# First two slots of an in-projection as three f32r products of rounded parts and rests

## The reference

```python
h = rms_norm(x, g_pre_mix[i])
proj = h @ w_in[i]
sb_q, sb_k, sb_v, q_lat, kv_lat, k_rope = jnp.split(proj, split_at, axis=-1)
...
cos, sin = rope_tables(positions, x.dtype)
```

## Time and profile before

| | us |
|---|---|
| median of 3 runs (lowest to highest) | 994.34 (993.92 to 997.03) |
| the profiled execution, its own time | 995.91 |
| the profiled execution, span from first to last instruction | 994.1 |
| PE busy | 813.6 (82%) |
| DVE, ACT, POOL busy | 331.9, 309.9, 143.9 |
| mean granted PE clock | 0.928 |

### The profile page before, as it was taken

How to read it: one execution, slowest core, us unless ns; L and a number is a source line. 1 busy time by engine, 2 the same in 40 slices (tenths; PEclk the granted TensorE clock), 3 DMA queues, 4 the chain that set the end, 5 groups by cost and what they waited for, 6 DMA issues and landing times.

```text
span 994.1 us, 12347 instructions
## 1 busy us (share of the span) xinstructions
PE 813.6 (82%) x5144; PEld 528.1 (53%) x5144; DVE 331.9 (33%) x700; ACT 309.9 (31%) x621; POOL 143.9 (14%) x153
## 2 busy tenths in 40 slices
PE   7998879999999999999889998767666775665854
PEld 5856447899997886687768542213112221221212
DVE  3306465667676545559531310001000000100001
ACT  2316355666665556645541300000100000000001
POOL 0011013344443005135400000000000000000000
PEclk9999989999999999999989999879989688889779
DMA  9932964454553566733809799999999999999994
GB/s 359 428 113 82 396 273 169 157 183 170 183 197 109 220 216 218 294 143 116 307 1 404 263 398 396 428 431 426 429 428 427 429 428 428 428 427 427 430 428 201
DMA packets 23677, 297.93 MB, mean 300 GB/s; under 512 B 2752, under 2 KB 3008, under 8 KB 5440
## 3 DMA queue, kind: packets, MB, share of 16 engines
q1 hardware_dynamic: 23616, 297.09, 74.1%
HBM read 296.03 MB, written 1.05 MB: 299 GB/s over the span
## 4 chain that ended last, share of the span: by engine, by line
PE 53%; DMA 33%; DVE 6%; ACT 5%; POOL 1%; issue 1%; SPq 0%; DVEq 0%; POOLq 0%
PE ps L186 53%; DMA ring<-in_exps 32%; ACT ar L200 1%; POOL ar L217 1%; DVE ar L206 1%; ACT yT L200 1%; DVE fr L206 1%; ACT ar L197 1%; DMA ring<-in_win 1%; DVE yT L214 0%; ACT fr L197 0%; DVE misc L596 0%; ACT sq L200 0%; DVE yT L206 0%; PE ps L619 0%
## 5 line engine op out<-in xcount | busy, mean ns | idle before, releaser
L186 PE MATMUL ps<-ring,sq 128*32 128x512 f32 x976 | 138.1, 703 | 71.0 <-DMA ring<-in_exps 70.7
L186 PE MATMUL ps<-ring,ar 128*32 128x512 f32 (+3 forms) x792 | 106.7, 629 | 51.6 <-DMA ring<-in_exps 44.5
L186 PE MATMUL ps<-fr 128*128 128x256 f32 (+1 forms) x852 | 144.9, 325 | 4.7 <-DVE fr L206 4.3
L186 PEld LDWEIGHTS ps<-fr 128*128 128x128 f32 x852 | 124.9, 190 | 20.3 <-DVE fr L206 4.1
L186 PEld LDWEIGHTS ps<-ring,sq 128*32 128x32 f32 x976 | 29.7, 119 | 169.1 <-DMA ring<-in_exps 113.3
L186 PE MATMUL ps<-hT,ring 128*128 128x256 f32 (+2 forms) x416 | 93.3, 385 | 6.8 <-DMA ring<-in_win 6.8
L206 DVE TENSOR_TENSOR ar<-ar,ps 128x512 f32<-128x512 f32 x9 | 6.2, 688 | 253.7 <-PE ps L186 253.7
L186 PEld LDWEIGHTS ps<-hT,ring 128*128 128x128 f32 (+2 forms) x416 | 78.1, 189 | 20.8 <-DMA ring<-in_win 6.8
L186 PEld LDWEIGHTS ps<-ring,ar 128*32 128x32 f32 (+1 forms) x792 | 28.0, 121 | 112.4 <-DMA ring<-in_exps 69.7
L186 PE MATMUL ps<-ar 128*128 128x512 f32 (+9 forms) x320 | 72.8, 462 | 14.8 <-DVE ar L206 8.9
L206 DVE TENSOR_TENSOR fr<-ring,fr 128x512 fp32r<-128x512 f32 x79 | 65.1, 842 | 44.2 <-ACT fr L197 44.0
(11 more groups left out here) (194 smaller groups left out, 931.8 us busy)
## 6 DMA issues: line engine op xcount, KB each, us to landing
ring<-in_exps SPq DMA_DIRECT2D x90, 2048.0 KB, 30.7
ring<-in_modw SPq DMA_DIRECT2D x12, 2048.0 KB, 8.2
ring<-in_wup SPq DMA_DIRECT2D x11, 2048.0 KB, 8.8
ring<-in_win SPq DMA_DIRECT2D x5, 2048.0 KB, 9.2
ring<-in_wdown SPq DMA_DIRECT2D x5, 2048.0 KB, 8.3
ar<-in_exps SPq DMA_DIRECT2D x3, 2048.0 KB, 12.4
ring<-in_wo SPq DMA_DIRECT2D x2, 2048.0 KB, 10.1
ring<-in_wgate SPq DMA_DIRECT2D x2, 2048.0 KB, 8.5
```

The source lines that it names most:

```text
L186: return pe(lambda e: e.matmul(o, l, r, start=start, stop=stop, skip_group_check=True), *waits, inc=inc)
```

## The change

The diff does four things. The 8 tiles of `hT` are each split into parts (`t_in`, into `fr` at 7680 and 9728). The weights of k-tiles 2 to 7 of slot 0 are split (`first_parts`; rests of even k on DVE, of odd k on POOL) and multiplied as three f32r products; k-tiles 0 and 1 stay f32. All 8 k-tiles of slot 1 are split (`in_parts`; rests of k 3 and 7 on POOL, the others on DVE) and multiplied so, all four column groups for each k. There are four pairs of buffers for weight parts, so parts of a fifth k-tile wait for the products of the first. The rope table, the squares and Silu move behind.

```diff
--- before.py
+++ after.py
@@ -306,13 +306,63 @@
         th = []
         for k in range(8):
             th.append(v_ts(tile(hT, k), tile(xT, k), col("g_pre_mix", k), None, ALU.mult, None, d_x[k // 4], d_g))
-        tsq = [a_fn(sq[:, 1024 * i:1024 * i + 1024], xT[:, 1024 * i:1024 * i + 1024], ACT.Square, d_x[i]) for i in range(2)]
-        t_silu = a_fn(silu_c, col("c", 0, 8), ACT.Silu, d_cols)
 
         def tiles_of(w, m, nt=8, ncol=512, width=128, src=None, toks=None, at=0):
             src, toks = (hT, th) if src is None else (src, toks)
             return [(w.ap(k * ncol + m, width), tile(src, k, at), toks[k]) for k in range(nt)]
 
+
+        rx0 = ar[:, rxo:rxo + S]
+        b = 0
+
+        def x_stats():
+            return wide_factor(0, [(tile(sq, k), tsq[k // 4]) for k in range(8)], 0, 1024, rx0)
+
+        IX, IW = (7680, 9728), [3072, 4096, 5120, 6144]
+        i_n, i_free = [0], [None] * 4
+
+        def split(src, hi, lo, low, *waits):
+            t = a_copy(hi, src, *waits)
+            return low(lo, src, hi.bitcast(F32), ALU.subtract, t)
+
+        def in_parts(src, low, *waits):
+            i = i_n[0] % 4
+            i_n[0] += 1
+            h, l = fr[:, IW[i]:IW[i] + 512], fr[:, IW[i] + 512:IW[i] + 1024]
+            return i, h, l, split(src, h, l, low, i_free[i], *waits)
+
+        def in_products(k, parts, places):
+            i, wh, wl, t_w = parts
+            xh, xl = (tile(fr, k, o) for o in IX)
+            for m, (o, width) in enumerate(places):
+                c = slice(128 * m, 128 * m + width)
+                mm(o, wh[:, c], xh, k == 0 and m % 2 == 0, False, t_w, t_in[k])
+                mm(o, wh[:, c], xl, False, False)
+                t = mm(o, wl[:, c], xh, False, k == 7, inc=int(m == len(places) - 1))
+            i_free[i] = t
+            return t
+
+        t_in, first = [], {}
+
+        def first_parts(k):
+            first[k] = in_parts(ring[:, 512 * k:512 * k + 512], p_tt if k % 2 else v_tt, d_w0[k // 2])
+
+        for k in range(8):
+            t_in.append(split(tile(hT, k), tile(fr, k, IX[0]), tile(fr, k, IX[1]), v_tt, th[k]))
+            if 2 <= k < 6:
+                first_parts(k)
+        tsq = [a_fn(sq[:, 1024 * i:1024 * i + 1024], xT[:, 1024 * i:1024 * i + 1024], ACT.Square, d_x[i]) for i in range(2)]
+        for k in range(8):
+            if k < 2:
+                for m in range(4):
+                    t = mm(bank(4 + m // 2, (m % 2) * S, (m % 2) * S + S), ring[:, 512 * k + 128 * m:512 * k + 128 * m + 128], tile(hT, k),
+                           k == 0 and m % 2 == 0, k == 7, d_w0[k // 2], th[k], inc=int(m == 3))
+            else:
+                t = in_products(k, first[k], [(bank(4 + m // 2, (m % 2) * S, (m % 2) * S + S), 128) for m in range(4)])
+                if k < 4:
+                    first_parts(k + 4)
+        freed[0] = t1 = t2 = t_first = t
+        t_silu = a_fn(silu_c, col("c", 0, 8), ACT.Silu, d_cols)
 
         R, R2, RS = slice(64, 96), slice(64, 128), slice(96, 128)
         pf, kk, an = ar[R2, rt:rt + S], ar[R2, rt + S:rt + 2 * S], ar[R2, rt + 2 * S:rt + 3 * S]
@@ -334,18 +384,7 @@
             t = v_ts(o, o, -3.1415925, None, ALU.max, None, t)
             t_tab.append(t)
 
-
-        rx0 = ar[:, rxo:rxo + S]
-        b = 0
-
-        def x_stats():
-            return wide_factor(0, [(tile(sq, k), tsq[k // 4]) for k in range(8)], 0, 1024, rx0)
-
-        for k in range(8):
-            for m in range(4):
-                t = mm(bank(4 + m // 2, (m % 2) * S, (m % 2) * S + S), ring[:, 512 * k + 128 * m:512 * k + 128 * m + 128], tile(hT, k),
-                       k == 0 and m % 2 == 0, k == 7, d_w0[k // 2], th[k], inc=int(m == 3))
-        freed[0] = t1 = t2 = t
+        t1 = t2 = t_first
         t_rx = x_stats()
         t_q = []
         for j, t in enumerate((t1, t2)):
@@ -367,14 +406,15 @@
 
         w = stream("win", 1)
         t_k = []
+        for k in range(8):
+            p = in_parts(w.ap(512 * k, 512), p_tt if k % 4 == 3 else v_tt, w.ready)
+            t = in_products(k, p, [(bank(6 + m // 2, (m % 2) * S, (m % 2) * S + S), 128) for m in range(4)])
+        w.free(t)
         for j in range(2):
             b = 6 + j
-            chain(bank(b, 0, S), tiles_of(w, 256 * j), w.ready)
-            t = chain(bank(b, S, 512), tiles_of(w, 256 * j + 128))
             o = ar[:, kT + 512 * j:kT + 512 * (j + 1)]
             read[b] = v_tt(by(o, S), by(bank(b), S), wide(rx0, 2), ALU.mult, t, t_rx)
             t_k.append(read[b])
-        w.free(t)
         rcol = misc[:, 4:6]
         for j in range(2):
             t = mm(ps[:, 1, j:j + 1], rx0[:, 128 * j:128 * j + 128], ones[:, 0:1], True, True, t_rx, inc=j)
@@ -663,10 +703,6 @@
 
         OX, OW = (0, 2048), [4096, 5120] + [7680 + 1024 * k for k in range(6)]
         o_n, o_free, wo, th, w_o = [0], [None] * 8, {}, [None] * 8, []
-
-        def split(src, hi, lo, low, *waits):
-            t = a_copy(hi, src, *waits)
-            return low(lo, src, hi.bitcast(F32), ALU.subtract, t)
 
         def out_low(k, t, low, *waits):
             hi, lo = (tile(fr, k, o) for o in OX)
```

## The result

The changed kernel takes 1002.71 us (median of 11 runs, 1000.66 to 1006.64), the kernel before 995.98 (median of 11, 993.77 to 1001.69). The ratio is 1.0070, 95% interval 1.0052 to 1.0088, so the change costs 5.2 to 8.8 us. The forecast was slower, by 5.7 us, at 1000.0 with a range to 1002.3; the measured median lies 0.4 us above that range.

The account below looks back on a forecast made before the run. It took PE to bound everything ahead of the transfer-bound expert layer, handing delays on. Terms -0.4 + 6.0 - 2.3 + 1.8 + 0.7 gave +5.8, by the exact mark +5.7: 994.34 + 5.7 = 1000.0 us, range 996.5 to 1002.3.

Parts of the forecast that it names:

- What bounds it, and that a shift is handed on: PE ahead of the transfer-bound expert layer: its shift at 40 us reaches the end one for one, or nearly.
- Term 1: Slot 0: products of parts start at 13.4 us with one POOL collision, sums of squares at 22.1 for 22.53, -0.4 us.
- Term 2: Start of slot 1: PE waits for weight parts queued behind the statistics on ACT and DVE, +6.0 us.
- The rival in which slot 1 doesn't wait: Slot 1's parts are ready when the sums end: -2.0 us, 992.3; chance 0.03.
- Term 3: Slot 1: 96 f32r products at 0.120 us each take 11.7 us against 13.98 in f32, -2.3 us.
- the rival at the floor of the columns: Both slots: 168 products at 0.109 us each take 1.8 us off, 998.2; chance 0.04.
- Term 4: Slot 1 behind PE's idle time: it starts at the low clock, +1.8 us.
- The rival without it: Slot 1: the clock stays up or falls too late to matter, +3.9 us, 998.2; chance 0.12.
- Term 5: End of slot 1: both banks' scalings stand between the last matmul and the scores, +0.7 us.
- The mark at the scores: First scores, 39.56 us before: what the change does to their start it does to the kernel; expected at 45.3.
- The last rival: More is lost: POOL and DVE collisions starting both slots, low-clock stretches falling worse, +8.5 us, 1002.8; chance 0.10.

Follow-up runs that it names:

- before_delayed: The kernel before with 18 f32 matmuls, read by nobody, put on PE ahead of the first scores: 1006.06 us, ratio 1.0092 to the kernel before.
- no_pool_slot0: The changed kernel with the rests of slot 0's weights all on DVE, none on POOL: 1003.03 us, ratio 1.0076 to the kernel before.
- changed_again: The changed kernel once more, unchanged, for a second profile: 1004.40 us in a single execution.
- slot1_f32: The changed kernel with slot 1 put back to 32 plain f32 matmuls, slot 0 keeping its parts: 997.46 us, ratio 0.9997 to the kernel before.
- filler: The changed kernel with 13 f32 matmuls, read by nobody, put on PE behind the statistics: 1001.70 us, ratio 1.0052 to the kernel before.
- early_parts: The changed kernel with the parts of slot 1's k-tiles 0 to 3 made ahead of the statistics: 998.93 us, ratio 1.0021 to the kernel before.

## Why the prediction was right in its steps and off at its end

- **What bounds it, and that a shift is handed on.** Right: before_delayed shows it by itself. (The shortest wait in the view behind the earlier trace rows is one of 0.3 us for DVE, not the 0.4 shown as such; none is for a transfer, as the forecast says.)
- **Term 1, slot 0, -0.4 us.** Measured on the means of three profiles: the sums start at 23.28 before (22.53, 24.19, 23.11) and at 22.74 after (23.54, 22.36, 22.33), -0.5. The mechanism, POOL in the way of DVE, is shown by no_pool_slot0, and how it falls varies: in changed_again the tiles of hT took 2.23 us but the rest of k-tile 2 only 0.68, and POOL's own second subtraction stretched to 4.46 us; in the first profile the rest took 1.75. I took one collision; there were one or two. The start at 13.4 that I took was met at 13.53 and 13.50, and missed at 14.71. That the term comes out so near is luck. slot1_f32, filler and early_parts have the same slot 0, and their products of parts start at 13.96, 14.88 and 14.98, the last two with the rest of k-tile 2 at 1.76 and 1.75 us: two collisions in three profiles of six, a start at 14.3 on the mean, 0.9 later than I took. On the means of these six and of four with the slot 0 of before (with before_delayed, 22.41) the sums start at 23.3 and 23.1: +0.3 us in place of -0.4. Three profiles of each kernel are too few to tell these from each other, since a start moves by more than 1 us between executions.
- **Term 2, the new wait, +6.0 us.** 8.05 us from the sums to slot 1 in place of 2.11 (24.64 - 22.53), so +5.94, in each of the three profiles. The rival in which slot 1 doesn't wait is out.
- **Term 3, products in place of f32, -2.3 us.** At full clock 11.78 us (filler) against 13.98: -2.2. The spacing of 0.120 us held. The page "TensorE: Matmul & The Clock Gate" of the Trainium skill, section "Back-to-back issue gap", gives its 109 ns for an isolated gap; this stream doesn't run at it, and the rival at the floor of the columns is out.
- **Term 4, the clock, +1.8 us.** 14.28, 13.26 and 13.38 us less 11.78: 2.5, 1.5 and 1.6, on the mean 1.9. The rival without it is out for this kernel, by the granted clock of 0.50 behind the wait in each of the three profiles. The price of 1.8 us was taken from the start of slot 0, where the windows grant 1.00; that it holds behind the wait is what filler shows.
- **Term 5, both scalings at the end, +0.7 us.** 1.55 us from the last product to the scores in place of 0.94: +0.6.
- **The sum, +5.7 us.** -0.5 + 5.9 - 2.2 + 1.9 + 0.6 = +5.7, and the means of the scores say 5.7, as they must, since the terms are pieces of the same profiles. With +0.3 for slot 0 it is +6.5. The measured whole, 7.0 us (5.2 to 8.8), is in keeping with both. Whether what lies between is more than chance stays open. The mark at the scores, read from one profile, tells the whole to some 3 us only: set against a mean start of 40.3 for before, the whole lies above the shift of the scores in eight of the nine kernels, by 0.2 to 3.3 us, and 1.1 us under it in filler.
- **The last rival, more is lost, +8.5 us.** Its 1002.8 is nearly the measured median, but on a base that was too low; the shift was 6.7 to 7.0. Its second collision came in slot 0 in three profiles of six, and at the start of slot 1 in none of the three of the changed kernel, which all took 8.05 us to it.
- **The step that failed** is the last one, "a shift doesn't depend on that, so I set it on the median: 994.34 + 5.7 = 1000.0". The shift doesn't, but the time does, and it took the base as known. The three runs behind 994.34 lay low: the 11 runs of which they are the first three gave 995.98, and the runs of the same kernel beside the experiments 997.28 (29 runs) and 996.71 (24 runs). Of the 2.7 us between 1000.0 and 1002.71, 1.6 are this base and 1.0 the shift, 6.7 us between the medians in place of 5.7. 995.98 + 5.7 is 1001.7. And the range was built of the terms and the rivals alone; it held nothing for a base that is known to 2 or 3 us, and the measured time lies 0.4 us outside. The profile that I made the sum on had its hint: its own execution took 995.91.

The first pair of profiles would have led the other way. It shows 7.86 us at the scores, 2.2 more than the forecast, and reads as though terms 1 and 4 had been too small by 1.4 and 0.7 us. The other profiles say that term 4 was not, and term 1 by about half of that.

## What to carry to other kernels

When an operation on PE is cut into parts that other engines must make, look where those parts stand in the queues of these engines, not only how long they take: 8 k-tiles of parts were cheap everywhere here, and their place behind one chain of statistics cost 5.9 us, plus 1.9 of clock for the idle PE, against 2.2 won in the slot. In slot 0 the products, shorter by 1.8 us, won nothing that can be told: the wait for their first parts, 1.2 to 2.6 us, took it. When a forecast is given as a time, give the base its own uncertainty, from as many runs as there are, and don't read the sign or size of a term of 2 us from one pair of profiles.

## What the hardware showed that I hadn't expected

- The windows grant 1.00 for the first 12 us in every profile, yet the 16 f32 instructions at the start of slot 0 take 5.10 to 6.45 us in place of 3.5. The slow start isn't in that column; it is read from the length of these instructions, and that it is the clock is inferred.
- How long PE runs slow after a start, and how long the granted clock stays at 0.50 (1.2 GHz) after a wait, differs between executions: the 64 instructions of an f32 slot 0 took 15.55 (before_delayed) to 17.09 us, the 96 products of slot 1 behind the wait 13.04 (no_pool_slot0) to 14.28. Over stretches A and B two executions of one kernel are up to 6.3 us apart, 2.6 of them by the clock in B.
- POOL holds up not only DVE's subtractions but its multiplications of one tile by a column: four tiles of hT took 2.15 to 2.23 us beside POOL and 1.14 without it (no_pool_slot0). The page "SBUF — State Buffer" of the Trainium skill, section "SBUF: two separate sides", calls the port pair of the two engines an exclusive lock, which for certain DVE operations one of them holds for a whole instruction; the 1.0 us that DVE lost beside one POOL subtraction of 1.27 to 1.43 agrees.
- POOL can be kept waiting over many instructions of DVE. In changed_again a POOL subtraction, 1.29 us alone, took 4.46:

```profile
12.44 4.46 POOL L217 TENSOR_TENSOR fr<-ring,fr 128x512 fp32r<-128x512 f32 x1 [1.25 <-ACT fr L197]
```

DVE worked without a gap until 15.75 meanwhile; the subtraction ended at 16.90, and the one that DVE took up at 15.94 lasted 1.52 us in place of 0.68. That reads as though POOL came to its turn only in DVE's pause, which no run tests.
